# Nine up-projection slabs of the feed-forward as seven block products, with weight sums on GpSimd

## The reference

```python
def conv_geglu_ffn(h, w_up, conv_w, w_down):
    up = causal_depthwise_conv(h @ w_up, conv_w)
    gate, val = jnp.split(up, 2, axis=-1)
    return (jax.nn.gelu(gate, approximate=True) * val) @ w_down
```

## Time and profile before

| what | value |
|---|---|
| median of three runs | 1811.91 us |
| profiled execution, its own time | 1812.99 us |
| its span, first to last instruction | 1811.2 us |
| TensorE busy | 1743.7 us, 96% |
| VectorE busy | 632.1 us, 35% |
| ScalarE busy | 290.1 us, 16% |
| GpSimd busy | 72.3 us, 4% |
| mean granted TensorE clock | 0.990 |
| first layer: first two up slabs | 1107.5 to 1137.0 us |
| first layer: up slabs 2 to 10 | 1137.0 to 1261.4 us |
| first layer: down-projection and the sums behind it | from 1261.4 us |

### The profile page before, as it was taken

The page is one execution under the profiler, slowest core; times in us unless marked ns, Lnnn a source line. Parts: engine busy times, 40 slices in busy tenths (PEclk is TensorE's granted clock), DMA queues, the critical chain, the costliest instruction groups (busy, mean ns, idle before and its releaser), DMA issues.

```text
span 1811.2 us, 23200 instructions
## 1 busy us (share of the span) xinstructions
PE 1743.7 (96%) x10024; PEld 1322.5 (73%) x10024; DVE 632.1 (35%) x1304; ACT 290.1 (16%) x452; POOL 72.3 (4%) x86
## 2 busy tenths in 40 slices
PE   6999899989999999999999999999999999999997
PEld 2447788884544545454798889888899898998887
DVE  3007433141111111110287535444047844454403
ACT  2003302030000000000124322000012432100001
POOL 4000000000000000000102200000000210000000
PEclk8999999999999999999999999999999999999999
DMA  9772313556999999999443023544334302254440
GB/s 349 266 275 94 139 47 111 203 201 288 428 428 428 428 428 427 427 427 428 144 166 114 12 83 96 184 147 174 122 112 141 109 31 93 94 181 145 139 163 24
DMA packets 116704, 375.66 MB, mean 207 GB/s; under 512 B 12714, under 2 KB 62226, under 8 KB 101136
## 3 DMA queue, kind: packets, MB, share of 16 engines
q1 hardware_dynamic: 115236, 373.54, 53.8%
q0 software_dynamic: 1216, 0.89, 0.2%
q10 hardware_dynamic: 172, 0.05, 0.0%
HBM read 373.41 MB, written 1.05 MB: 207 GB/s over the span
## 4 chain that ended last, share of the span: by engine, by line
PE 75%; DMA 16%; DVE 7%; ACT 1%; issue 1%; SPq 0%; DVEq 0%
PE PS L552 39%; DMA ring<-in_moe_w_dram 14%; PE PS L865 8%; PE PS L1320 6%; PE PS L1287 3%; PE PS L1262 3%; PE PS L1329 2%; PE PS L896 2%; PE PS L773 2%; PE PS L977 1%; DMA ring<-in_w_in_dram 1%; DVE arena L2239 1%; PE PS L838 1%; PE PS L587 1%; PE PS L986 1%
## 5 line engine op out<-in xcount | busy, mean ns | idle before, releaser
L552 PE MATMUL PS<-arena,ring 128*128 128x256 f32 (+1 forms) x2496 | 561.7, 387 | 2.7 <-DMA ring<-in_w_in_dram 1.7
L552 PEld LDWEIGHTS PS<-arena,ring 128*128 128x128 f32 x2496 | 473.7, 191 | 84.9 <-issue 18.0
L865 PE MATMUL PS<-ring,arena 128*64 128x512 f32 x1024 | 225.1, 593 | 7.9 <-DMA ring<-in_moe_w_dram 6.7
L865 PEld LDWEIGHTS PS<-ring,arena 128*64 128x64 f32 x1024 | 74.2, 137 | 155.6 <-issue 155.5
L896 PE MATMUL PS<-ring,arena 128*64 128x512 f32 x512 | 113.4, 595 | 0.5 <-ACT arena L1631 0.5
L1320 PE MATMUL PS<-arena,ring 128*128 128x256 f32 x512 | 110.8, 379 | 0.0
L2239 DVE SCALAR_TENSOR_TENSOR arena<-PS,colsL,arena 128x255 f32<-128x255 f32 (+2 forms) x248 | 108.1, 477 | 4.4
L1320 PEld LDWEIGHTS PS<-arena,ring 128*128 128x128 f32 x512 | 97.3, 190 | 13.2
L2237 DVE TENSOR_SCALAR arena<-PS,colsL 128x256 f32<-128x256 f32 x112 | 49.0, 479 | 152.9 <-PE PS L552 138.7
L552 PE MATMUL PS<-arena 128*128 128x128 f32 (+3 forms) x704 | 87.4, 282 | 6.8 <-DVE arena L2450 3.3
L2157 DVE TENSOR_TENSOR arena<-arena,PS 128x512 f32<-128x512 f32 x16 | 16.9, 1053 | 215.0 <-PE PS L865 215.0
(11 more groups left out here) (377 smaller groups left out, 1618.2 us busy)
## 6 DMA issues: line engine op xcount, KB each, us to landing
ring<-in_moe_w_dram SPq DMA_DIRECT2D x96, 2048.0 KB, 16.5
ring<-in_w_in_dram SPq DMA_DIRECT2D x23, 2048.0 KB, 8.3
ring<-in_ffn_w_up_dram SPq DMA_DIRECT2D x44, 1024.0 KB, 7.1
ring<-in_w_mod_dram SPq DMA_DIRECT2D x24, 1024.0 KB, 9.8
ring<-in_ffn_w_down_dram SPq DMA_DIRECT2D x10, 2048.0 KB, 7.8
ring<-in_w_out_dram SPq DMA_DIRECT2D x4, 2048.0 KB, 7.8
ring<-in_w_gla_br_dram SPq DMA_DIRECT2D x2, 2048.0 KB, 8.5
ring<-in_w_o_dram SPq DMA_DIRECT2D x2, 2048.0 KB, 8.7
```

The lines of the kernel that those rows point to most:

```text
L552: last = mm(PS[:, b, place] if not isinstance(place, tuple) else PS[place[0], b, place[1]], lhsT(k), rhs(k), start=(k == 0), stop=(k == K ...
L865: last = mm(PS[e * SLOTS:(e + 1) * SLOTS, 4 + j, :], hg[:, k, e * SLOTS:(e + 1) * SLOTS], expert_slab(2 * j + e, KT)[:, k, :], start=(k == ...
```

## The change

For slabs 2 to 10 of each layer the product of weights and tokens is split into blocks. With the weights of a slab as A and the tokens as B, A11 and A12 are the gate columns over the first and second half of the features, A21 and A22 the value columns; B11 and B12 are the first half of the features for the first and second 128 tokens, B21 and B22 the second half. The four results take eight block products directly. The change uses seven, of sums (the Winograd form of Strassen's scheme): four sums of weights, four sums of tokens, and results that share partial sums.

- GpSimd forms the four weight sums of every slab (four `tensor_tensor` of 128x1024, each a quarter of a slab) into `wsum`, three deep, in the scratch part of `ring`; and once per layer the four token sums `tsum`. It starts a layer's sums when `oc_ready` tells that the scratch is free, and each slab when its weights have landed.
- TensorE does a product as 8 matmuls of 128x128 weights by 128 tokens (`product`). Of slab `j` it does one, two, five and six, then, beside the next slab, seven, four and three. Bank A collects one, six, seven and four, bank D five and three, bank B two.
- ScalarE copies bank A after product one and after six, and bank D after five, into `held`; the growing bank is read at these steps. It copies the last state of bank A too.
- VectorE adds `held` and PSUM three times per slab into `upc`, and the convolution reads `upc` in SBUF where it read PSUM.
- TensorE may begin product four only when VectorE has taken the state before it (`fourth_read`). In VectorE's program that addition stands behind both convolutions of the slab before.
- A slab's place in `ring` is given back when product four and the weight sums are done.
- The last slab's products are interleaved with the first down-projection slab.

The diff, cut to its core:

```diff
+        wsum = ringflat[:, 3 * SLAB:].rearrange("p (b n q) -> p b n q", b=3, n=4)
...
-                for j in range(2, FFT // 2):
-                    w2 = up_slab(j)
-                    for v in range(2):
-                        tiles(ph3, ("up", j, v), [(half(i), lambda k, i=i: w2[:, v, k, i * P:(i + 1) * P], h)
-                                                  for i in range(2)], KT)
+                def product(b, w4, b4, first=False, end=False):
+                    for i in range(2):
+                        for k in range(4):
+                            last = mm(PS[:, b, th(i)], w4[:, k, th(i)], b4[:, k, :], start=(first and i == 0 and k == 0),
+                                      stop=(end and i == 1 and k == 3), skip_group_check=True)
+                    last.then_inc(S("up_products"), 1)
...
+                def five_and_six(j):
+                    b = ph3.hold(pe, ("D", j))
+                    w4 = summed(j, 1)
...
+                    product(b, w4, tsum[:, 0], first=True)
+                    w4 = summed(j, 2)
+                    pe.wait_ge(S("held_copied"), held_due(j, 1))
+                    product(ph3.place(("A", j)), w4, tsum[:, 1])
+                def four(j):
+                    pe.wait_ge(S("fourth_read"), due("fourth_read", j - FIRST_SUMMED + 1))
+                    product(ph3.place(("A", j)), raw(j, 1, 1), tsum[:, 3], end=True)
...
+                for j in range(FIRST_SUMMED, FFT // 2):
+                    one_and_two(j)
+                    if j > FIRST_SUMMED:
+                        seven(j - 1)
+                    five_and_six(j)
+                    if j > FIRST_SUMMED:
+                        four(j - 1)
+                        three(j - 1)
...
+                        elif SL3[before][0] == "up":
+                            n = SL3[before][1] - FIRST_SUMMED + 1
+                            sp.wait_ge(S("up_products"), products_due("four", SL3[before][1]))
+                            sp.wait_ge(S("weights_summed"), due("weights_summed", 4 * n))
...
+                for j in range(FIRST_SUMMED, FFT // 2 + 2):
+                    if j - 2 >= FIRST_SUMMED:
+                        act.wait_ge(S("value_conv"), due("value_conv", j - 2 - FIRST_SUMMED + 1))
+                        gelu(j - 2)
...
+                            A(held[:, n, j % 2], two(ph3.place((at, j))), ACT.Copy).then_inc(S("held_copied"), 1)
...
+                for j in range(FIRST_SUMMED, FFT // 2 + 2):
+                    m = j - 2
+                    if m >= FIRST_SUMMED:
+                        dve.wait_ge(S("held_copied"), held_due(m, 3))
+                        dve.wait_ge(S("up_products"), products_due("three", m))
+                        b = ph3.place(("D", m))
+                        V.tensor_tensor(upc[:, m % 2, 0:2, th(1)], held[:, 2, m % 2], two(b), ALU.add).then_inc(psum_free[b], 1)
+                        ph3.freed(dve, ("D", m))
+                        dve.wait_ge(S("gated"), due("gated", m - 1))
+                        up_conv(m, 0, [upc[:, m % 2, i, :] for i in range(2)]).then_inc(S("value_conv"), 1)
...
+                        link(up_conv(m, 1, [upc[:, m % 2, 2 + i, :] for i in range(2)]))
+                    if FIRST_SUMMED < j <= FFT // 2:
+                        dve.wait_ge(S("held_copied"), held_due(j - 1, 2))
+                        dve.wait_ge(S("up_products"), products_due("seven", j - 1))
+                        V.tensor_tensor(upc[:, (j - 1) % 2, 2:4, th(1)], held[:, 1, (j - 1) % 2],
+                                        two(ph3.place(("A", j - 1))), ALU.add).then_inc(S("fourth_read"), 1)
...
+                def sum_weights(j):
...
+                    pool.wait_ge(ll[i % 3], total3[i % 3] * l + loads3[i])
+                    if m >= 3:
+                        pool.wait_ge(S("up_products"), products_due("three", j - 3))
...
+                    nc.gpsimd.tensor_tensor(to[0], a21, a22, ALU.add).then_inc(S("weights_summed"), 1)
+                    pool.wait_ge(S("weights_summed"), due("weights_summed", 4 * m + 1))
+                    nc.gpsimd.tensor_tensor(to[1], to[0], a11, ALU.subtract).then_inc(S("weights_summed"), 1)
+                    nc.gpsimd.tensor_tensor(to[2], a11, a21, ALU.subtract).then_inc(S("weights_summed"), 1)
+                    pool.wait_ge(S("weights_summed"), due("weights_summed", 4 * m + 2))
+                    nc.gpsimd.tensor_tensor(to[3], a12, to[1], ALU.subtract).then_inc(S("weights_summed"), 1)
```

More of the change, by code:

```diff
@@ L238, in bank, with hold @@
                 return b
+            def hold(self, pe, key):
+                b = self.banks[len(self.at) % len(self.banks)]
+                if bank_uses[b]:
+                    pe.wait_ge(psum_free[b], bank_uses[b])
+                bank_uses[b] += 1
+                self.at[(self.layer, key)] = (None, b, bank_uses[b])
+                return b
             def read(self, eng, key):
@@ L430, in build @@
         rsb = A3.view[:, 14336:14336 + 2048]
+        tsum = A3.view[:, 17920:17920 + 2048].rearrange("p (n k c) -> p n k c", n=4, k=4)
+        held = A3.view[:, 14336:14336 + 1536].rearrange("p (n b i c) -> p n b i c", n=3, b=2, i=2)
+        upc = cat.rearrange("p k t -> p (k t)").rearrange("p (b j t) -> p b j t", b=2, j=4)
+        wsum = ringflat[:, 3 * SLAB:].rearrange("p (b n q) -> p b n q", b=3, n=4)
+        FIRST_SUMMED = 2
+        LAST_UP = FFT // 2 - 1
+        order = [(n, FIRST_SUMMED) for n in ("one", "two", "five", "six")]
+        for j in range(FIRST_SUMMED + 1, LAST_UP + 1):
+            order += [("one", j), ("two", j), ("seven", j - 1), ("five", j), ("six", j), ("four", j - 1), ("three", j - 1)]
+        order += [(n, LAST_UP) for n in ("seven", "four", "three")]
+        product_at = {step: n + 1 for n, step in enumerate(order)}
         outt = sc3.rearrange("p k t -> p (k t)").rearrange("p (t d) -> p t d", t=TT)
@@ new lines, in one_and_two, with seven @@
+                def one_and_two(j):
+                    b = ph3.hold(pe, ("A", j))
+                    product(b, raw(j, 0, 0), hT[:, 0:4, th(0)], first=True)
+                    b = ph3.hold(pe, ("B", j))
+                    product(b, raw(j, 0, 1), hT[:, 4:8, th(0)], first=True, end=True)
+                def seven(j):
+                    pe.wait_ge(S("held_copied"), held_due(j, 3))
+                    product(ph3.place(("A", j)), summed(j, 3), tsum[:, 2])
+                def five_and_six(j):
+                    b = ph3.hold(pe, ("D", j))
+                    w4 = summed(j, 1)
+                    if j == FIRST_SUMMED:
+                        pe.wait_ge(S("tokens_summed"), due("tokens_summed", 4))
+                    product(b, w4, tsum[:, 0], first=True)
+                    w4 = summed(j, 2)
+                    pe.wait_ge(S("held_copied"), held_due(j, 1))
+                    product(ph3.place(("A", j)), w4, tsum[:, 1])
@@ L1310, in _, with down_slab @@
                 bt = ph3.bank(pe, ("end_sums", 0))
                 banks = [ph3.bank(pe, ("down", g)) for g in range(3)]
+                def down_slab(j, fs):
+                    w = slab3("down", j // 4, 4, D)
+                    pe.wait_ge(S("gated"), due("gated", (j + 4) // 2))
+                    for f in fs:
+                        for k in range(4):
+                            last = mm(PS[:, banks[f // 2], half(f % 2)], w[:, k, f * P:(f + 1) * P], gated[:, j + k, :],
+                                      start=(f % 2 == 0 and j + k == 0), stop=False, skip_group_check=True)
+                    return last
@@ L1312, in _ @@
+                down_slab(0, range(4))
+                seven(LAST_UP)
+                down_slab(0, range(4, 6))
+                four(LAST_UP)
+                three(LAST_UP)
                 if l + 1 == LAYERS:
@@ L1314, in _ @@
                 banks.append(ph3.bank(pe, ("down", 3)))
[L1315 to L1322 removed]
+                down_slab(0, range(6, KT)).then_inc(S("down_read"), 1)
+                for j in range(4, 16, 4):
+                    down_slab(j, range(KT)).then_inc(S("down_read"), 1)
                 rest = [(slab3("down", k // 4, min(4, FFT - 4 * (k // 4)), D), k) for k in range(16, FFT)]
@@ L2626 @@
+                sum_weights(FIRST_SUMMED)
+                sum_tokens()
+                for j in range(FIRST_SUMMED + 1, FFT // 2):
+                    sum_weights(j)
 _INS = ['x', 'c', 'ctx', 'c_ctx', 'w_mod', 'b_mod', 'norm1_g', 'norm2_g', 'w_in', 'gla_a2_f', 'gla_ab_f', 'gla_a2_b',
```

78 lines of the change are left out of this document (60 added, 18 removed).

## The result

| kernel | median, us | ratio to before, 95% interval |
|---|---|---|
| before | 1811.99 | |
| changed | 1840.71 (1837.81 to 1844.2, 4 runs) | 1.0158 (1.0138 to 1.0179) |

The change makes the kernel 28.7 us slower; 1835.5 was predicted. The profiled execution of the changed kernel is the fastest of its four, 1837.81 us with a span of 1836.0, 24.8 us above the span before. These runs scatter more than those of before (6.4 against 2.2 us), and the two layers of one execution differ.

The account below looks back on a forecast made before the run. TensorE's matmuls were taken to bound slabs 2 to 10. Matmul gain, late steps and start, 2 x (-11.7 + 22.5 + 1.0) = +23.6 us on 1812.99, gave 1836.6, as median 1835.5; range 1790 to 1850.

Parts of the forecast that it names:

- Small matmuls: Slabs 2 to 10: seven products of 1.787 us replace 13.81 us per slab, gaining 1.30 per slab, 11.7 us per layer.
- The engines hold each other when VectorE takes both inputs from SBUF: GpSimd sums and VectorE's SBUF convolution and gating exclude each other for whole instructions, 14.0 to 15.1 us per slab.
- The late steps: Steps (TensorE, product three's end to the next slab's) 5, 7, 9: product four 7.5 us late each, 22.5 per layer.
- the march: Step-by-step walk through the up-projection, engines alternating by single instructions, four 2.2 us sums before the addition in late steps.
- step 5: First late step: fourth convolution pair reached at 5.9 us, addition ends at 16.5, step lasts 20 us.
- The 14.0 us per slab: Exclusive VectorE and GpSimd time per slab, 15.1 us less handover savings, against TensorE's 12.5 and the old 13.81.
- some 23 as a sign of being right: Sign that the forecast holds: TensorE's matmul busy time down by some 23 us.
- The start: Slab 2's sums beside the second token half's normalisation delay TensorE: 1 us per layer taken, range 0.6 to 4.
- The sum: Whole kernel, both layers: 2 x (-11.7 + 22.5 + 1.0) = +23.6 us, median 1835.5.
- A: Rival: engines hardly hold each other where it counts; -19 to -23 us, about 1790; chance 0.15.
- B: Rival: engines take turns by pairs in slabs 2 to 10; -4.7 us per layer, 1802.5; chance 0.16.
- C: Rival: late in every step, 5.9 us stall in six steps; +55 us, 1866; chance 0.12.

Follow-up runs that it names:

- run 1: Changed kernel with GpSimd's four weight sums per slab cut to 64 of 1024 columns (feed-forward not computed rightly): 1789.17 us, ratio 0.9871.
- run 2: Kernel before with the changed kernel's GpSimd weight and token sums added but unused, convolution still reading PSUM: 1821.57 us, ratio 1.0053.
- run 6: Changed kernel with VectorE's addition that releases product four placed between the two convolutions instead of behind both: 1840.46 us, ratio 1.0155.
- run 7: Changed kernel with that addition between the convolutions, and ScalarE's gelu behind the copies of products one and five: 1832.54 us, ratio 1.0116.
- run 10: Changed kernel with token sums first, sums in halves, early addition, value half's first convolution tap on ScalarE, gelu behind copies: 1790.63 us, ratio 0.9879.

## Why the prediction was right

*Small matmuls.* 1.30 us per slab from 0.216 and 0.112 us per record. Run 1 shows it undisturbed: 960 records in 107.36 us, and 22.6 us under the kernel before in all.

*The engines hold each other when VectorE takes both inputs from SBUF.* Shown by run 1 against the changed kernel, and by run 2, where the same sums stand beside the convolution from PSUM for nothing and yet hold the gating. The Trainium skill's rule (SBUF — State Buffer, Who interferes with whom) also names tensor_scalar in a two-port mode; the trace agrees that tensor_scalar from SBUF is held, 626 against 348 ns. Which mode it ran in no trace shows.

*The late steps.* Predicted in 5, 7 and 9, 7.5 us each. Measured in the first layer in just these, 6.5 (0.55 and 5.94), 3.1 and 8.0 us, 17.6 together for 22.5. The second layer had two, 10.5 us together. So the term was too large by 5 and 12 us, 17 together. Two numbers in it were off: the march put four sums of 2.2 us into every late step, and the timelines show three, two and four of 2.05. (The march is also 0.4 to 1.1 us short of its own terms in step 5: 5.9, then two pairs or three, four sums and the addition, are 16.9 to 17.6 and not 16.5.) A load that lands a little later finds fewer of the convolution's operations in front of the addition. The landing was taken as one number, and that it sets the order of the turns is my reading of the timelines; no run moved a landing. The 14.0 us per slab that the engines were to share did not by themselves make this kernel slow: in steps 4 to 9 of the first layer GpSimd stands idle for 2.46 to 10.41 us before each load, and VectorE for 1.69 to 6.39 us before each addition of bank D. What costs is where the sums stand.

*The clock.* This term was missing. Over the matmuls of slabs 2 to 10, the first layer is 136.5 us (131.1 to the first down-projection record, and three products of 1.79) against 124.3: +12.2. Of it -11.7 is the gain and +17.5 the waits, so +6.4 is matmuls at the lower clock. The second: +3.8 = -11.7 + 10.5 + 5.0. That is 11.4 us that no term of the sum held. It and the clock at the start are why TensorE's busy time fell by 11.2 us only, where the prediction named some 23 as a sign of being right.

*The start.* Taken as 1 us, in a range to 4. It is 5.0 in the first layer (34.5 us from product to product against 29.5 before) and 5.7 in the second. The waits are 2.8 and 3.7 of these, the rest is clock. In the trace two sums stand between the first three of the eight operations, as the upper bound had it, and the first operation waits for one already in progress:

```profile
1119.83 7.51 DVE L2315 SCALAR_TENSOR_TENSOR arena<-xT,colsL,arena 128x128 f32<-128x128 f32 x8 [2.11 <-ACT arena L1898]
1121.13 2.40 POOL L2784 TENSOR_TENSOR ring<-ring 128x1024 f32<-128x1024 f32 x1
1123.50 2.39 POOL L2786 TENSOR_TENSOR ring<-ring 128x1024 f32<-128x1024 f32 x1
```

Eight operations that took 2.19 us take 7.51. The step that failed here is the choice of 1 us; a GpSimd instruction that waits gets in after every single VectorE instruction, the rule that the march used, and used there it gives 4. The waits came to 2.8 and 3.7 us; the clock behind them is in no term.

*The sum.* Per layer -11.7 + 22.5 + 1.0 was predicted. Measured: -11.7 + 17.5 + 6.4 + 5.0 and -11.7 + 10.5 + 5.0 + 5.7, +17.2 and +9.5, together 26.7; the profiled span grew by 24.8, so 1.9 were gained outside these stretches. Against the 23.6 of the forecast the waits were 17.0 too many, the clock 11.4 and the start 8.7 too few. So the mechanism was right, but that the sum came within 3.1 us is partly luck: two underestimates and one overestimate met. The other three executions are 1.5 to 6.4 us slower than the profiled one, which is how the median comes to 28.7.

*The rivals.* A (1790) is what run 1 shows without holding. B, turns by pairs, fell with the 7.97 us of four operations, in which three sums stand, and with the 9.98 us, in which four do. C did not come: steps 4, 6 and 8 of the first layer have no wait.

What stays open: how the hardware decides whose turn it is. The traces show turns after single instructions; they don't show that this must be so.

## What to carry to other kernels

Before giving an idle engine work beside a busy one, ask for each operation of both where its inputs lie: here moving the convolution's source from PSUM to SBUF made every one of its operations one that a GpSimd sum can hold, and neither engine's busy share told of it (39% and 14%). Ask next which of these operations stand before the one that the busiest engine waits for, and how many of the other engine's instructions can fall among them. When the waits are in a good order, add up what the two engines share per round and compare it with the round, for a lag that grows by some us per round is met in the end; reordering gained nothing in run 6, 8 us in run 7 and 6 us in run 10. Long instructions on the slower side are best cut in pieces (17 us here), and a third engine with room is the place for single-input work (9 us with the order mended). Count the clock as well: a few long waits cost more than many short ones of the same sum.

## What the runs showed of the hardware that I had not expected

- TensorE's clock is 0.50 behind idle stretches of 5.94 and 7.95 us and back at 1.00 within about 8 us. Behind 3.12 us it stayed at 1.00, and yet it fell behind 3.81 us, behind 0.96 and 1.86 us close together, and in run 6 behind a stretch of 2.08 us (0.67 from 1194.80 to 1198.00). No length of a single stretch parts the two cases here. In the changed kernel this costs some 11 us beside the waits themselves, and 4 more at the start.
- In all, the same sums as eight instructions of 512 columns hold VectorE for less than as four of 1024 (gating 962 against 1467 ns on average, tensor_scalar 565 against 626, the scalar_tensor_tensor from SBUF together 92.8 against 91.8 us, so no less), though alone they take more (8 x 1.27 = 10.2 against 9.4 us).
- VectorE pays for the turns and GpSimd hardly does: each sum that gets in costs VectorE 2.05 us, while the sums of step 5 begin 2.42, 2.37 and 2.48 us apart, where four with nothing held between them (from 1153.12) begin 2.43, 2.30 and 2.31 apart.
- Loads land after 5.1 to 8.7 us before the change; two layers of one execution show different patterns of waits (steps 5, 7, 9 and steps 5, 8), and the changed kernel's runs scatter over 6.4 us where before they kept within 2.2.
